# Row sums of the mixing weights by VectorE and memory in place of TensorE, and the next weights loaded before the bias

## What is computed

```python
# layer A
a, g, z = split(h @ w_in); c = a * sigmoid(g); y = causal depthwise conv_31(c)
out = (silu(layernorm(y)) * silu(z)) @ w_out
# layer B
u, v = gelu(h @ w_uv); z = h @ w_z; v = layernorm(v)          # v * ln_g + ln_b per channel
mixed[i] = sum_j ws[group, i, j] * v[j] + s_bias[group, i]    # 128-frame chunks, 8 groups, masked 64-frame blocks
out = ((u * mixed) * silu(z)) @ w_out
```

## Time and profile before

| | us |
|---|---|
| median of 3 runs | 2219.44 (2218.34 to 2219.84) |
| the profiled execution, own time | 2218.88 |
| its span in the profile | 2217.1 |
| TensorE busy | 2205.6 |
| VectorE busy | 1596.1 |
| ScalarE busy | 968.1 |
| GpSimd busy | 358.1 |

### The profile page before, as it was taken

One profiled execution on the slowest core, in us unless ns is written; L12 is line 12 of the kernel. 1 busy time (PEld: TensorE's weight loads), 2 busy tenths in 40 slices (PEclk: granted clock), 3 DMA queues, 4 the chain that ended last, 5 costly groups with the idle time before them and its releaser, 6 DMA issues.

```text
span 2217.1 us, 29967 instructions
## 1 busy us (share of the span) xinstructions
PE 2205.6 (99%) x11815; PEld 1942.0 (88%) x11815; DVE 1596.1 (72%) x1990; ACT 968.1 (44%) x1455; POOL 358.1 (16%) x517
## 2 busy tenths in 40 slices
PE   9999999999999999999999999999999999999998
PEld 7888899999888888888888888888889999998887
DVE  6789999997788988999986227852296666667321
ACT  7443333333453225665665125542236656666210
POOL 2111111111221112121110101210112121120000
PEclk9999999999999999999999999999999999999999
DMA  8555666564444313334346426352213333236321
GB/s 302 190 153 153 154 180 189 148 171 120 174 176 162 110 70 110 111 101 125 106 131 217 148 103 221 135 180 88 86 62 93 104 98 107 86 101 241 142 95 38
DMA packets 135436, 303.75 MB, mean 137 GB/s; under 512 B 18176, under 2 KB 54784, under 8 KB 133760
## 3 DMA queue, kind: packets, MB, share of 16 engines
q1 hardware_dynamic: 106192, 203.00, 27.6%
q0 software_dynamic: 28960, 98.57, 15.5%
q10 hardware_dynamic: 144, 0.26, 0.0%
HBM read 223.40 MB, written 78.75 MB: 136 GB/s over the span
## 4 chain that ended last, share of the span: by engine, by line
PE 98%; DMA 1%; DVE 0%; ACT 0%; SPq 0%; issue 0%; POOL 0%; DVEq 0%; POOLq 0%
PE PS L2357 31%; PE PS L2359 31%; PE PS L2358 31%; PE PS L2608 2%; PE PS L2364 1%; PE PS L2363 1%; PE PS L2450 1%; PE PS L2472 1%; DMA rawb<-wb_out_in 0%; DMA B22r<-wb_uz_in 0%; DMA raw<-wa_in_in 0%; PE PS L2459 0%; PE PS L2690 0%; PE PS L2613 0%; DVE S3l L1667 0%
## 5 line engine op out<-in xcount | busy, mean ns | idle before, releaser
L1729 DVE SCALAR_TENSOR_TENSOR acc<-cp,cw,acc 128x513 f32<-128x513 f32 (+3 forms) x464 | 366.9, 791 | 14.3
L2357 PE MATMUL PS<-HAh,Wh 128*128 128x512 f32 (+2 forms) x960 | 340.4, 355 | 3.7 <-DVE HAl L1672 2.2
L2358 PE MATMUL PS<-HAl,Wh 128*128 128x512 f32 (+2 forms) x960 | 338.7, 353 | 0.0
L2359 PE MATMUL PS<-HAh,Wl 128*128 128x512 f32 (+2 forms) x960 | 338.6, 353 | 0.0
L2357 PE MATMUL PS<-Vh,HBh 128*128 128x512 f32 x512 | 199.6, 390 | 0.0
L2359 PE MATMUL PS<-Vh,HBl 128*128 128x512 f32 x512 | 199.2, 389 | 0.0
L2358 PE MATMUL PS<-Vl,HBh 128*128 128x512 f32 x512 | 199.2, 389 | 0.0
L2357 PEld LDWEIGHTS PS<-HAh,Wh 128*128 128x128 f32 x960 | 180.4, 188 | 20.1 <-DVE Wl L1667 4.2
L2357 PE MATMUL PS<-Wbh,s7h 128*128 128x512 f32 x500 | 195.3, 391 | 0.0
L1756 DVE SCALAR_TENSOR_TENSOR over<-pair,cg,over 128x512 f32<-128x512 f32 (+1 forms) x240 | 189.9, 791 | 7.4
L2359 PE MATMUL PS<-Wbh,s7l 128*128 128x512 f32 x500 | 194.6, 389 | 0.0
(11 more groups left out here) (255 smaller groups left out, 5227.0 us busy)
## 6 DMA issues: line engine op xcount, KB each, us to landing
raw<-wa_in_in SPq DMA_DIRECT2D x48, 512.0 KB, 4.7
Wl<-wa_in_in POOLq DMA_DIRECT2D x39, 512.0 KB, 5.7
rawv<-wb_v_in SPq DMA_DIRECT2D x64, 256.0 KB, 5.0
QWr<-wb_uz_in SPq DMA_DIRECT2D x64, 256.0 KB, 2.6
v_scratch<-vb POOLq DMA_DIRECT2D x64, 256.0 KB, 2.6
vt<-v_scratch SPq DMA_DIRECT2D x32, 512.0 KB, 3.9
s_scratch<-m POOLq DMA_DIRECT2D x32, 512.0 KB, 4.0
rawb<-wb_out_in SPq DMA_DIRECT2D x28, 512.0 KB, 8.3
```

The costliest lines, as they stand in the source:

```text
L1729: return nc.vector.scalar_tensor_tensor(out=out, in0=src, scalar=w, in1=first, op0=ALU.mult, op1=ALU.add)
L2357: nc.tensor.matmul(out, wh, xh, start=start, stop=False, skip_group_check=seeded)
L2358: nc.tensor.matmul(out, wh, xl, start=False, stop=False, skip_group_check=seeded)
L2359: return nc.tensor.matmul(out, wl, xh, start=False, stop=stop, skip_group_check=seeded)
```

## The change

A second copy of the weights, `ws_i` as [i, group, j], comes in as an input. SyncE loads it in unit 8 of stage A into free room (`wsi`, 512 KB). In unit 12 VectorE sums over j with two reductions: partitions 0 to 63 over the first 64 values of each group, partitions 64 to 127 over all 128. The result `wsum` is [128, 8]. In unit 14 GpSimd writes it to memory as one row of 1,024 numbers; the order there is group by group, so every number goes to a place of its own. Each gating stage loads that row, broadcast to 128 partitions, as `rsb` (`rsb_load`). The products `u_row_sums` and the copy `u_sums` go away; mixing 0 now itself waits for the banks and the mask. In half 0, SyncE issues B12, B22 and B11 of block 1 ahead of `vt_load(0)` and the bias.

```diff
@@ build
+    rs_d = nc.dram_tensor("row_sum_scratch", [1, GROUPS * P], fp32).ap()
+        wsum = g("wsum", [P, GROUPS])
+        wsi = at(m_at + 13312, "wsi", [P, GROUPS, P])
@@ quad_order
-            order = [("M1", 0), ("rs", 0)] + [(m, 0) for m in ("M6", "M2", "M7", "M5")]
+            order = [("M1", 0)] + [(m, 0) for m in ("M6", "M2", "M7", "M5")]
@@ sync
+            def rows_load():
+                sp.dma_start(wsi[:, :, :], ws_i).then_inc(u_rows, 16)
+
+            def rsb_load(h):
+                if h == 0:
+                    sp.wait_ge(u_sums, 16)
+                else:
+                    sp.wait_ge(v_mm, V_DONE[h])
+                sp.dma_start(kp(rsb[:, :, :]), rs_d.to_broadcast([P, GROUPS * P])).then_inc(u_sbb, 16)
...
             def q_stage(h):
+                ahead = ("B12", "B22", "B11") if h == 0 else ()
+                for b in ahead:
+                    q_load(h, b, 1)
                 vt_load(h, 0)
                 if h == 0:
                     sp.wait_ge(q_slo, s_split(h, "S3"))
                     sbb_load(h)
+                rsb_load(h)
                 for j in range(KB):
                     if j + 1 < KB:
                         for b in ("B12", "B22", "B11", "B21"):
-                            q_load(h, b, j + 1)
+                            if j > 0 or b not in ahead:
+                                q_load(h, b, j + 1)
                         vt_load(h, j + 1)
...
+                if n == 8:
+                    rows_load()
@@ gpsimd, after the stores of unit n
+                if n == 14:
+                    pool.wait_ge(u_rows, 18)
+                    nc.gpsimd.dma_start(rs_d.rearrange("o (g p) -> p (o g)", p=P), wsum[:, :],
+                                         allow_slow_non_contiguous=True).then_inc(u_sums, 16)
@@ vector
+                if (n, c) == (12, 0):
+                    row_sums()
...
-            def u_sums(h):
-
-                dve.wait_ge(u_rsmm, h + 1)
-                if h == 0:
-                    dve.wait_ge(q_slo, s_split(h, "S3"))
-                nc.vector.tensor_copy(kp(rsb[:, :, :]), banks(MIX)).then_inc(u_rsb, 1)
+            def row_sums():
+                half = P // 2
+                dve.wait_ge(u_rows, 16)
+                nc.vector.tensor_reduce(wsum[0:half, :], wsi[0:half, :, 0:half], mybir.AxisListType.X, ALU.add)\
+                    .then_inc(u_rows, 1)
+                nc.vector.tensor_reduce(wsum[half:P, :], wsi[half:P, :, :], mybir.AxisListType.X, ALU.add).then_inc(u_rows, 1)
@@ u_add_bias
-                    dve.wait_ge(u_sbb, 16 * (h + 1))
-                    dve.wait_ge(u_rsb, h + 1)
+                    dve.wait_ge(u_sbb, 32 * (h + 1))
@@ vector, q_stage
-                u_sums(h)
@@ tensor
-            def u_row_sums(h):
-                pe.wait_ge(u_mask, h + 1)
-                for i in range(2):
-                    pe.wait_ge(v_gel, v_last(h, MIX + i))
-                    last = nc.tensor.matmul(PS[:, MIX + i, :], one.to_broadcast([P, P]), kp(wst[:, 4 * i:4 * (i + 1), :]),
-                                            start=True, stop=True)
-                last.then_inc(u_rsmm, 1)
@@ u_mixing
                 if j == 0:
-                    pe.wait_ge(u_rsb, h + 1)
-                    if h == 1:
-                        pe.wait_ge(v_gel, v_last(h, 5))
+                    pe.wait_ge(u_mask, h + 1)
+                    for b in range(5 if h == 1 else MIX, 8):
+                        pe.wait_ge(v_gel, v_last(h, b))
```

More of the change, by code:

```diff
@@ L98, in conv_plan, with build @@
     return steps, read, ends
-def build(nc, x, x_t0, x_t1, wa_in, wa_out, wb_v, wb_uz, wb_out, hist, conv_w, chan_par, pre_g, post_g, b_gb, ws_t, s_bias,
+def build(nc, x, x_t0, x_t1, wa_in, wa_out, wb_v, wb_uz, wb_out, hist, conv_w, chan_par, pre_g, post_g, b_gb, ws_t, ws_i, s_bias,
           consts, y_out, conv_out, v_out):
@@ L391, in build @@
             ("hi", "lo", "mm", "gel", "silu", "mu", "mz"))
-        u_ws, u_mask, u_rsmm, u_rsb, u_sbb = (sem(f"u_{n}") for n in ("ws", "mask", "rsmm", "rsb", "sbb"))
+        u_ws, u_mask, u_rows, u_sums, u_sbb = (sem(f"u_{n}") for n in ("ws", "mask", "rows", "sums", "sbb"))
         u_ldv, u_sub, u_vn, u_vo, u_add, u_mix, u_mev, u_sst, u_vst = (sem(f"u_{n}") for n in
@@ L2656, in q_stage @@
                         u_mixing(h, i)
-                    elif m == "rs":
-                        u_row_sums(h)
                     else:
@@ L2839 @@
         "ws_t": np.asarray(b_w_s)[0].transpose(2, 0, 1),
+        "ws_i": np.asarray(b_w_s)[0].transpose(1, 0, 2),
         "s_bias": np.asarray(b_s_bias)[0].reshape(1, GROUPS * P),
```

## The result

The changed kernel takes **2227.27 us** (median of 5, 2227.05 to 2227.53), the kernel before beside it 2218.79 (5, 2218.34 to 2219.84). The ratio is 1.0037, 95% interval 1.0023 to 1.0051: the medians are 8.5 us apart, where 0.75 was forecast. The profiled execution has 2227.53, span 2225.7, mean clock 0.998.

What follows compares the result with a forecast made beforehand. TensorE's queue was taken as the bound. A 2.05 us stall in stage A less 1.3 us gained in the first gating stage gave +0.75 us on 2218.88, 2219.6; the median 0.56 above made 2220.1 us, range 2217.7 to 2222.7.

Steps and rivals of the forecast that it cites:

- What bounds the kernel: Whole kernel: time is TensorE's queue length, busy 2205.6 of 2217.1 us; only work removed or waits added there count.
- First gating stage, 1.3 us: First gating stage: row-sum products removed and next weights loaded ahead together gain 1.3 us.
- The split into 0.8 and 0.5: First gating stage: 0.8 us from removing products, 0.5 us from loading block 1's weights ahead.
- rival 4: First gating stage: `vt` lands late behind the moved loads, the 1.3 us are gone, 2221.4 us; chance 0.08.
- Nothing either: First gating stage: the 512 KB broadcast of spread sums arrives before VectorE asks for it, costing nothing.
- Second gating stage, gain 0: Second gating stage: the 1.72 us of products removed are waited out at M7 for VectorE's S3 split; gain 0.
- Stage A, the failed step: Stage A, unit 17: TensorE waits 2.05 us for low weights, 0.95 from reductions plus 1.1 from the write.
- Bounds 0 (absorbed) and 4; I take 1.1: Stage A, GpSimd's queue: delay by the write of 1,024 single numbers, taken as 1.1 us, between 0 and 4.
- The reductions' 0.95: Stage A, unit 17: VectorE's 1.75 us of reductions less 0.8 us cover leave 0.95 us of stall.
- rival 1: Stage A's cover holds: cheap reductions, absorbed writes, or faster landing of unit 17's load; 2218.1 us; chance 0.27.
- so it is paid once: Stage A: later units add no stall, since TensorE is itself later by unit 17's stall.
- Rival 2: Stage A: small writes hold GpSimd's queue for w us, 2219.1 + w; chance 0.08 for w beyond 4.7.

Runs made afterwards that it cites:

- e2: Changed kernel without the write of the row sums, load and reductions kept, bias row loaded in their place: 2220.33 us, ratio 1.0009.
- e5: Changed kernel with the sums written as 128 runs of 32 bytes, read back with a stride: 2221.17 us, ratio 1.0011.
- e13: Changed kernel writing one column, 128 single numbers placed 512 bytes apart, bias row in place of the sums: 2220.91 us, ratio 1.0011.
- e14: Changed kernel writing all 1,024 single numbers 512 bytes apart, bias row in place of the sums: 2221.38 us, ratio 1.0012.
- e9: Changed kernel with the write cut to 512 single numbers side by side, bias row in place of the sums: 2226.54 us, ratio 1.0035.
- e12: Changed kernel writing one column, 128 single numbers side by side, bias row in place of the sums: 2225.08 us, ratio 1.0029.
- e6: Changed kernel with sums written as 128 runs of 32 bytes, reductions moved to unit 25 and write to unit 27: 2220.02 us, ratio 1.0006.

## Why the prediction was wrong

- **What bounds the kernel:** right. The time is TensorE's queue and its waits, and stage A was the place with little to spare.
- **First gating stage, 1.3 us:** right in sum, 1.39 measured, and in its signs (0.76 us behind ScalarE's copy, and no idle between mixing 0 and block 1). The split into 0.8 and 0.5 was a wrong way to see it: the move alone gives 0.75, and the removal without the move costs 1.55, so that the sum came out right is in part luck. `vt` behind the moved loads costs nothing, as worked out (rival 4): ScalarE now waits 1.36 us for it, but begins its scaling 9.65 us behind the stage's first product, as before. "Nothing either", said of the spread sums, holds only because the weights now go ahead of them.
- **Second gating stage, gain 0:** right. The segment from the M1 of that stage to the end is no shorter (566.97 against 566.74). M6 stands 0.90 us there, which the prediction had left to M7, and M7 0.75.
- **Stage A, the failed step.** Place, instruction and chain were right: unit 17, waiting for its low weights' DMA. The sum was "1.75 - 0.8 = 0.95" and 1.1 on top. The issue moved by 192.99 - 190.63 = 2.36 us, 0.28 of it the later start, so 2.08 for the reductions (1.95 on VectorE itself). The cover was 0.8, as worked out. The term that failed is the write: "Bounds 0 (absorbed) and 4; I take 1.1". The landing went from 6.6 to 12.6 us, so it was **6.0**. 2.36 + 6.0 - 0.8, less the 0.28 by which TensorE started later too, is the 7.3 of the trace. The bound of 4 came from copies with runs of 120 bytes, 30 numbers each. No row of the trace before showed single numbers from different partitions written side by side; a bound by the nearest rows was no bound. ("Half of one 120-byte copy" is 1.0 by its own 2.0, not 1.1, and the sum ends at 2220.2 in place of 2220.1; neither matters.)
- **The reductions' 0.95** was too much as well. Without the write (e2) unit 17 lost 0.5 us: the low weights, issued some 2 us later, landed after 5.5 us in place of 6.6, which rival 1 had named as possible. Measured against e2, the write held that load for 12.6 - 5.5 = 7.1 us.
- **A term that was missing:** the clock. A wait of 7.3 us is followed by products at 0.50 of the clock, 1.6 us more. The sum had only the wait.
- **"so it is paid once":** wrong in general. e2, e5, e13 and e14 pay in unit 17 (0.3 to 0.9 us) and again before `o_transpose` in unit 44 (1.8 to 2.0 us), where VectorE bounds the end of stage A. The text looked only at the low weights as the way from VectorE to TensorE. The changed kernel doesn't show it, as it is later than that already.
- **Rival 2 was the true one**, by its own formula: 2219.1 + w gives 2225.1 with w = 6.0, and 1.6 for the clock makes 2226.7 of the 2227.3 measured. It was given 0.08 because of the bound. The Trainium skill (DMA: Bandwidth & Descriptors, rules for kernel authors, on strided last dimensions) names this pattern as one to avoid, and its advice, a contiguous last dimension, leaves 0.3 us of the wait for low weights (e5). The reason that it gives, one descriptor per element, is the smaller part here: 1,024 elements set apart landed in 5.2 us.

## What to carry to other kernels

A DMA of a few KB is not cheap because it is small: look at where its pieces fall. If neighbouring addresses get single numbers from many partitions, give every partition a run of its own and let the reader take the stride, and put the transfer where everything issued in the next 10 us, on any queue, has that much room. When work is added to an engine that has no pauses, follow its queue to the end of the stage and look at each hand-over to the bounding engine, not only at the first; and cost a wait of several us on TensorE with the slow products behind it (1.6 to 2.9 us here).

## What the runs showed that was not expected

- A write of 4-byte numbers side by side holds other transfers too, also those of another queue: SyncE's load of 512 KB took 11.3 us in place of 3.6, with the DMA engines at 0 to 35 GB/s for 8 us. 128 numbers (0.5 KB) do nearly the same (landing 9.4); set 512 bytes apart they land in 3.6.
- TensorE's granted clock: in profiled executions it fell to 0.50 behind waits of 7.3, 6.4, 5.8 (e9), 4.9 (e12) and 4.6 us. What that costs doesn't go by the wait: unit 17 lost 1.6 us to it behind the longest, 2.9 behind 6.4 and 5.8, and 2.1 behind 4.9. Behind e6's wait of 2.31 us it was 0.89 and then 0.69 in the two stretches of 4 us around and after it, and unit 44 took 16.50 us where e2, which waited 1.72 us for the same thing at a clock of 1.00, took 14.28.
- VectorE's reduction costs what an add or a copy of its input does: 0.67 us for 512 elements a partition, 1.22 for 1,024, on 64 partitions.
